# Pool product on two buffers with its low part one step later, and a fourth open unit in the attention output stage

## The reference

```python
# layer 0, four groups of 256 channels, windows 2, 4, 8, 16
u, gate = jnp.split(h @ w_in, 2, axis=-1)
pooled, new_hist = multiscale_pool(u, hist, hist_pos)
z = jnp.einsum('btgc,gcd->btgd', pooled, w_grp).reshape(B, T, POOL_WIDTH) * scale
y = (z * jax.nn.silu(gate)) @ w_out
# layer 1, 16 heads of 64, 4 key/value heads, window 128 in chunks of 64, with sinks
q, k, v, gate = jnp.split(h @ w_in, ...)
o = band_attend(q, k, v, qpos, kpos, sinks)
y = (o * jax.nn.silu(gate)) @ w_out
# both: x = x + gate_i(c) * y, with h = rms_norm(x) * (1 + scale_i(c)) + shift_i(c)
```

## Time and profile before

| | |
|---|---|
| median of three runs | 1714.47 us |
| the profiled execution's own time | 1710.07 us |
| its span, first to last instruction | 1708.1 us |
| mean granted TensorE clock | 0.964 |
| TensorE matmul busy | 1595.4 us, 9083 instructions |
| VectorE (DVE) busy | 866.5 us |
| ScalarE (ACT) busy | 747.4 us |
| GpSimd (POOL) busy | 420.2 us |

### The profile page before, as it was taken

The page is one execution under the profiler, slowest core; times in us unless marked ns, Lnnn a source line. Parts: engine busy times, 40 slices in busy tenths (PEclk is TensorE's granted clock), DMA queues, the critical chain, the costliest instruction groups (busy, mean ns, idle before and its releaser), DMA issues.

```text
span 1708.1 us, 27931 instructions
## 1 busy us (share of the span) xinstructions
PE 1595.4 (93%) x9083; PEld 1361.7 (80%) x9083; DVE 866.5 (51%) x2194; ACT 747.4 (44%) x1658; POOL 420.2 (25%) x403
## 2 busy tenths in 40 slices
PE   5899999999999999988888899999999999999998
PEld 3789987777777777788877788888788887888876
DVE  2555434433442444246666534677436765367751
ACT  3434332223222322246565543665545665456552
POOL 0333420011001100234434541233312333122331
PEclk8899999999999999999889889999999999999998
DMA  7777686556656655563434445433454334553323
GB/s 271 281 256 257 231 293 231 211 211 228 234 191 246 210 206 184 214 227 127 146 114 149 173 148 201 162 135 124 173 189 157 124 139 147 210 175 125 125 72 126
DMA packets 167605, 316.90 MB, mean 186 GB/s; under 512 B 21359, under 2 KB 88255, under 8 KB 167214
## 3 DMA queue, kind: packets, MB, share of 16 engines
q1 hardware_dynamic: 167470, 315.12, 52.7%
HBM read 240.96 MB, written 74.31 MB: 185 GB/s over the span
## 4 chain that ended last, share of the span: by engine, by line
PE 80%; DVE 6%; issue 4%; ACT 4%; DMA 1%; POOL 1%; SPq 0%; DVEq 0%; POOLq 0%; ACTq 0%
PE ps_u L832 65%; PE ps_o L1060 3%; PE ps_t L1033 3%; PE ps_s L1014 2%; PE ps_s L1015 2%; PE ps_s L863 1%; DMA work<-in_x_prompt_dram 1%; ACT work L1634 1%; DVE ps_u L1215 1%; ACT ps_u L1529 1%; PE ps_t L1073 1%; DVE ps_o L1393 1%; POOL work L1768 1%; DVE acc L1407 1%; PE ps_o L875 1%
## 5 line engine op out<-in xcount | busy, mean ns | idle before, releaser
L832 PE MATMUL ps_u<-h_all_hi,w_hi 128*128 128x512 f32 (+2 forms) x1440 | 525.2, 365 | 11.3 <-DVE acc L1224 6.3
L832 PE MATMUL ps_u<-h_all_lo,w_hi 128*128 128x512 f32 (+2 forms) x1440 | 515.6, 358 | 0.0
L832 PE MATMUL ps_u<-h_all_hi,w_lo 128*128 128x512 f32 (+2 forms) x1440 | 515.1, 358 | 0.0
L832 PEld LDWEIGHTS ps_u<-h_all_hi,w_hi 128*128 128x128 f32 x1440 | 279.8, 194 | 64.8 <-issue 17.8
L832 PEld LDWEIGHTS ps_u<-h_all_hi,w_lo 128*128 128x128 f32 x1440 | 278.9, 194 | 36.2
L832 PEld LDWEIGHTS ps_u<-h_all_lo,w_hi 128*128 128x128 f32 x1440 | 279.4, 194 | 34.4
L832 PE MATMUL ps_u<-y_hi,w_hi 128*128 128x512 f32 (+1 forms) x640 | 236.1, 369 | 12.8 <-POOL y_lo L1747 6.9
L832 PE MATMUL ps_u<-y_hi,w_lo 128*128 128x512 f32 (+1 forms) x640 | 230.3, 360 | 0.0
L832 PE MATMUL ps_u<-y_lo,w_hi 128*128 128x512 f32 (+1 forms) x640 | 230.1, 360 | 0.0
L1215 DVE TENSOR_TENSOR ps_u<-ps_u,rstd_b 128x512 f32<-128x512 f32 (+1 forms) x180 | 107.1, 595 | 208.1 <-PE ps_u L832 200.9
L1768 POOL TENSOR_TENSOR work<-work,recip 128x512 f32<-128x512 f32 (+2 forms) x136 | 132.9, 998 | 256.5 <-DVE recip L1380 256.5
(11 more groups left out here) (197 smaller groups left out, 2268.9 us busy)
## 6 DMA issues: line engine op xcount, KB each, us to landing
w_hi<-w_hi_kept SPq DMA_DIRECT2D x156, 512.0 KB, 3.6
w_lo<-w_lo_kept SPq DMA_DIRECT2D x156, 512.0 KB, 4.5
w_hi_kept<-w_hi SPq DMA_DIRECT2D x52, 512.0 KB, 2.7
w_lo_kept<-w_lo SPq DMA_DIRECT2D x52, 512.0 KB, 4.3
chunks<-in_ada_w_dram SPq DMA_DIRECT2D x32, 512.0 KB, 5.7
w_raw<-in_pool_w_in_dram SPq DMA_DIRECT2D x16, 512.0 KB, 5.6
w_raw<-in_attn_w_in_dram SPq DMA_DIRECT2D x16, 512.0 KB, 4.9
work<-in_x_prompt_dram SPq DMA_DIRECT2D x12, 512.0 KB, 6.0
```

The lines of the kernel that those rows point to most:

```text
L832: last = nc.tensor.matmul(out, w, x, start=(i == 0), stop=(i == n - 1))
```

## The change

The change has two parts.

*Pooling product.* The product for m = 1 is written to `sq`, that for m = 0 stays in `acc`. The subtraction that gives `y_lo` leaves step `E1` and becomes step `E2`, placed behind the `E1` of the following z unit. The wait of a z unit for the halves of the previous one is gone.

*Attention output stage.* Units get a bank by a rotation of their own, and the fourth unit opened in an attention output stage goes to the first bank of `ps_s`; in part 0 the fifth goes to the second. The plan opens four units (five in part 0) on slices 0 to 5 before the last item is through. Before it opens the fourth unit, TensorE waits until the scores have been read; the next stage's first use of `ps_s` waits for the readout of these units. A call that moved weight splits ahead (`split_to`) is kept for layer 0 alone there.

```diff
+            u = len(self.units)
+            if kind == "out" and more["layer"] and len(self.opened) in self.extra_banks(p):
+                bank = len(self.opened)
+            else:
+                bank = self.rotation
+                self.rotation = (self.rotation + 1) % 3
...
+    def extra_banks(self, p):
+
+        return (3,) if p else (3, 4)
...
                 for u in self.group(p, j, "z", n=2 * g + m, g=g, m=m):
                     self.project(u)
-                    s.extend(late)
+                    s.extend(late + lower)
+                    lower = [("E2", u - 1)] if late[0][0] == "E1" else []
                     late = [("E1", u)]
-            s.extend(late)
+            s.extend(late + lower + [("E2", late[0][1])])
...
+        top = 3 + len(self.extra_banks(p)) if layer else 3
...
-                for i in range(3):
+                for i in range(top):
                     self.project(order[i], done[i])
                     s.append(("E1", order[i]))
-                    self.split_to(j + AHEAD)
+                    if layer == 0:
+                        self.split_to(j + AHEAD)
...
-        plan = [(0, 0, 6), drain[0], (1, 0, 6), drain[1], (2, 0, 4), drain[2], (2, 4, 6)]
+        plan = [(0, 0, 6), drain[0], (1, 0, 6), drain[1], (2, 0, 6), drain[2], (3, 0, 6)]
         if p == 0:
-            plan.append(drain[3])
-        plan += [(0, 6, 7), drain[-1], (1, 6, 7), (2, 6, 7)]
+            plan += [drain[3], (4, 0, 6)]
+        plan += [(0, 6, 7), drain[-1], (1, 6, 7), (2, 6, 7), (3, 6, 7)]
...
+        def z_buf(u):
+
+            return sq if u["m"] else acc
...
-                    if u["u"] >= 3:
-                        v = units[u["u"] - 3]
+                    if u["bank"] >= 3:
+                        if k_from == 0 and u["bank"] == 3:
+                            claim("s", *[(x_new, x["nth_out"]) for x in units if x["s"] == u["s"] and x["bank"] >= 3])
+                    elif u["prev"] is not None:
+                        v = units[u["prev"]]
...
-                        if u["nth_z"] > 1:
-                            dve.wait_ge(yz_hi, u["nth_z"] - 1)
-                            dve.wait_ge(yz_lo, u["nth_z"] - 1)
-                        V.scalar_tensor_tensor(out=acc[:, c0:c0 + w], in0=bank[:, 0:w], scalar=half_ps[:, u["n"]:u["n"] + 1],
+                        V.scalar_tensor_tensor(out=z_buf(u)[:, c0:c0 + w], in0=bank[:, 0:w], scalar=half_ps[:, u["n"]:u["n"] + 1],
                                                in1=silu_g[:, i, c0:c0 + w], op0=ALU.mult, op1=ALU.mult).then_inc(y_ready, 1)
-                        dve.wait_ge(yz_hi, u["nth_z"])
-                        dve.wait_ge(y_ready, u["nth_z"])
-                        V.tensor_tensor(y_lo[:, u["n"], c0:c0 + w], acc[:, c0:c0 + w], y_hi[:, u["n"], c0:c0 + w].bitcast(F32),
-                                        ALU.subtract).then_inc(yz_lo, 1)
...
+                    if k == "z":
+
+                        dve.wait_ge(yz_hi, u["nth_z"])
+                        dve.wait_ge(y_ready, u["nth_z"])
+                        V.tensor_tensor(y_lo[:, u["n"], c0:c0 + w], z_buf(u)[:, c0:c0 + w], y_hi[:, u["n"], c0:c0 + w].bitcast(F32),
+                                        ALU.subtract).then_inc(yz_lo, 1)
```

More of the change, by code:

```diff
@@ L98, in __init__ @@
         self.stage = 0
+        self.rotation, self.last_in = 0, {}
         for p in range(PARTS):
@@ L141, in group @@
         for b, (c0, w) in enumerate(self.blocks(p)):
-            self.units.append(dict(u=len(self.units), s=self.stage, p=p, j=j, kind=kind, b=b, c0=c0, w=w, **more))
-            made.append(len(self.units) - 1)
+            u = len(self.units)
[4 more added lines that the diff above has]
+                self.rotation = (self.rotation + 1) % 3
+            if kind == "out" and more["layer"]:
+                self.opened.append(u)
+            self.units.append(dict(u=u, s=self.stage, p=p, j=j, kind=kind, b=b, c0=c0, w=w, bank=bank, prev=self.last_in.get(bank), **more))
+            self.last_in[bank] = u
+            made.append(u)
         self.last_unit[j] = made[-1]
@@ L221, in pool @@
                     s.append(("PL", p, g, 0))
-            late = []
+            late, lower = [], []
             for i in range(2):
@@ L275, in out_units @@
             us = self.group(p, j, "out", n=n, layer=layer)
-            fresh = us if len(order) >= 3 else us[3 - len(order):] if len(order) + len(us) > 3 else []
+            fresh = us if len(order) >= top else us[top - len(order):] if len(order) + len(us) > top else []
             before = len(order)
             order.extend(us)
-            if before < 3 <= len(order):
-                done = [0, 0, 0]
+            if before < top <= len(order):
+                done = [0] * top
                 for x in plan:
@@ L289, in out_units @@
                     if i == 0 and k0 == 0:
-                        self.split_to(j + (1 if p else 2))
-                for i in range(3):
+                        self.split_to(self.units[order[0]]["j"] + 3)
+                for i in range(top):
                     self.project(order[i], done[i])
                     s.append(("E1", order[i]))
-                    self.split_to(j + AHEAD)
+                    if layer == 0:
+                        self.split_to(j + AHEAD)
             for u in fresh:
@@ L546, in bank_of @@
         def bank_of(u):
-            return ps_u[u["u"] % 3][:, shifts(u):512]
+            return ps_u[u["bank"]][:, shifts(u):512] if u["bank"] < 3 else ps_s[:, u["bank"] - 3, :]
         def shifts(u):
@@ L936, in _ @@
                         pe.wait_ge(w_fetched[j % RING], 32 * fetches(j))
-                    bank = ps_u[u["u"] % 3]
+                    bank = ps_u[u["bank"]] if u["bank"] < 3 else ps_s[:, u["bank"] - 3, :]
                     slot = j % RING
@@ L1212, in _ @@
                         if p == 0 and u["b"] == 0:
-                            V.tensor_copy(wb[:, u["n"], :], ps_u[u["u"] % 3][:, 0:SHIFT])
+                            V.tensor_copy(wb[:, u["n"], :], ps_u[u["bank"]][:, 0:SHIFT])
                         dve.wait_ge(rb_ready, u["s"] + 1)
@@ L1556, in _ @@
                         act.wait_ge(y_ready, u["nth_z"])
-                        A(y_hi[:, u["n"], c0:c0 + w], acc[:, c0:c0 + w], ACT.Copy).then_inc(yz_hi, 1)
+                        A(y_hi[:, u["n"], c0:c0 + w], z_buf(u)[:, c0:c0 + w], ACT.Copy).then_inc(yz_hi, 1)
                     else:
```

3 lines of the change are left out of this document (2 added, 1 removed).

## The result

The changed kernel takes 1699.57 us at the median of four runs, beside 1714.25 for the kernel before (now also of four, hence not the 1714.47 above): a ratio of 0.9922, 95% interval 0.9902 to 0.9943. The forecast was 1705.0, within 1697 to 1712. A second comparison, further down, gave 0.9935 (0.9920 to 0.9950). The forecast's ratio, 0.9945, lies just outside the first interval and inside the second.

What follows compares the result with a forecast made beforehand. TensorE bounds the kernel, matmuls busy 93% of the span, so only its idle time and clock losses could shrink. Terms -8.2 - 4.3 - 3.1 + 6.1 = -9.5 us, from 1714.5 to 1705.0 us, range 1697 to 1712.

Steps and rivals of the forecast that it cites:

- Stage 0: Pooling z units: waits behind DVE's multiply go, three gaps of 2.09 us plus 1.9 of the fourth, together -8.2 us.
- Part 0: Attention's part 0: additional early matmuls fill the gaps, -4.3 us, and the clock holds, -3.1 us.
- Parts 1 to 3: Attention's later parts: +1.5 us each from less idle but a fetch stall, plus clock losses; together +6.1 us.
- the open point: Stage 0: second z multiply taken as free beside POOL's split, like L1215 at 0.44 us; if held, no gain.
- The fourth gap: Stage 0, before the output units: a 1.97 us wait, gain bounded by nothing and 2 us, taken as 1.9.
- the first rival: Stage 0: the DMA chain swallows the z gain, giving 2 to 3 of 8.2 us, about 1711; chance 0.2.
- The third 0.3: Part 0, third gap before the products with v: 18 more matmuls (2.25 us) leave 0.3 us of idle.
- The forecast counted 3.1: Part 0: the half-speed clock from 991.3 to 997.6 would hold instead, -3.1 us, bounds 0 and -3.9.
- 1.6 us before slice 7: Attention parts 1 to 3: TensorE idle of 1.6 us stays, from the end of slice 6 until slice 7 can start.
- 3.1 us of stall behind twelve matmuls: Attention parts 1 to 3, after slice 7: TensorE stands 3.1 us until the fifth weight tile lands.
- one fall of 1.7 us in each part: Attention parts 1 to 3: a clock loss of 1.7 us in every part, behind gaps of 1.6 and 3.1 us.
- what it counts as faster: Whole kernel faster than 1711.1 us: the forecast, the second rival and half of the first, given chance 0.82.

Runs made afterwards that it cites:

- A second comparison: The unaltered whole change measured again beside other kernels: 1705.30 us beside 1715.43 for the kernel before the change, ratio 0.9935.
- after: First profiled execution of the whole change against the kernel before it; median 1699.57 us beside 1714.25, ratio 0.9922.
- experiment 1: Only the z part of the change, on the kernel before with its three open units in attention: 1703.13 us beside 1713.06, ratio 0.9945.
- 2: Whole change, but additional open units in part 0 alone; parts 1 to 3 open three as before: 1695.56 us beside 1713.06, ratio 0.9894.
- Experiment 3: Whole change, but the fourth unit's 18 early matmuls in parts 1 to 3 are spread later: 1689.77 us beside 1713.06, ratio 0.9865.
- 5: The whole change run again, unaltered, against the kernel before: 1705.30 us beside 1715.43, ratio 0.9935.
- experiment 6: Whole change, but part 0 of attention opens four units instead of five: 1706.08 us beside 1715.43, ratio 0.9941.
- before: Profiled execution of the kernel without the change; median 1714.25 us in the first comparison.
- 4: Whole change with two buffers, but each y_lo right behind its multiply on VectorE as before: 1710.43 us beside 1713.06, ratio 0.9987.
- 7: Whole change with the old VectorE order, and the weight tile's split moved behind the group's last y_lo: 1709.41 us beside 1715.43, ratio 0.9966.
- Experiment 8: Kernel of Experiment 3 with each pool stage's third and fourth x tile loads earlier on SyncE's queue: 1684.70 us beside 1715.43, ratio 0.9824.
- 9: Kernel of Experiment 8, plus first loads of later output stages moved ahead of the first x_mid store: 1673.86 us beside 1713.16, ratio 0.9766.
- experiment 10: Kernel of 9, but products with the weights' upper half go first and the lower half is awaited behind them: 1668.20 us beside 1713.16, ratio 0.9731.

## Why the prediction came out

**The sum holds better than one execution shows.** Stage 0 with the new z order: 184.11, 181.69, 181.06, 179.68, 181.33 and 181.40 us (after, experiments 1 to 3, 5, 6), on average 181.5, against 188.57 before (and 188.50 with the old order in 4): -7.0 for a forecast of -8.2. Part 0 with five units: 297.58, 297.84, 297.75, 299.86 and 297.94 (after, 2 to 5), 298.2 on average against 305.20 and 304.60 (before, 1): -6.7 for -7.4. Parts 1 to 3 with the fourth unit as in the change: 666.45, 667.95, 672.19, 669.70 and 672.00 (after, 4 to 7), 669.7 against 665.37, 665.57 and 664.00 (before, 1, 2): +4.7 for +6.1. Together -9.0, and -9.5 was forecast. The median of the first comparison is 14.7 us lower, that of the second 10.1; the profiled executions differ by 11.7. The old order stands in few executions (two, two and three for the three stretches), and executions of one order differ by up to 4.4 us in stage 0 and 5.7 in parts 1 to 3, so the last microsecond of each difference means little.

**z: right, with one term too large.** Whether the multiply is held beside POOL's split had been the open point, and it hardly arose. In no execution, before or after, does a z multiply start beside a split: in the new order the second one is on its way 0.23 us before the split begins. It ends in its usual 0.49 us, and TensorE does not wait. That a multiply which starts behind the split's begin would also go through is still told only by L1215 in the earlier trace rows. The fourth gap was put at 1.9 of 0 to 2. It goes too, but the wait for x grows from 1.44 us to 2.4 to 4.2 (six executions, 2.9 on average), so 0.5 is left of it. This is the first rival's mechanism in small. It does not swallow the rest. Experiment 8 shows the cause, which I had named only in passing: the x load's late place on SyncE's queue.

**Part 0: right.** The idle went to 0.34, 0.58, nothing and 0.40 us for forecasts of 0.3, 0.8, 0.3 and 0.8, and the clock held. (The third 0.3 does not follow from the forecast's own terms: 2.25 us of matmuls cover a gap of 1.23 in full.) With 1.83 us of idle (experiment 6) its fall costs 1.7 us; with the gaps of up to 2.08 before it cost 5.1, and 3.4 in experiment 1, which has the old order there. The forecast counted 3.1.

**Parts 1 to 3: idle and stall right, the clock a mean of unlike cases.** 1.6 us before slice 7 was forecast and 1.63 measured; 3.1 us of stall behind twelve matmuls and 3.27, 2.85 and 2.89 measured (3.2 on average over the fifteen stalls of the five executions). I had counted one fall of 1.7 us in each part, 5.1 in all. After had one; the other four executions with the same order lost 5.1, 8.5, 6.8 and 8.5 us. The old order lost 3.4, 5.1 and 5.1. On average that is 6.1 against 4.5, and the difference is the 1.6 us of the forecast's sum (5.1 less 3.5). Of the fifteen stalls three left the clock up, six cost 1.7 us and six 3.4, and which did what does not follow their lengths: 3.44 us left it up, 2.92 cost 3.4. What decides it in a given execution stays open. The profiled execution of after is a lucky case. That such luck explains all that the first comparison gained beyond the forecast was not shown. The stretches hold falls of the clock in other places too, so the 1.4 us between +4.7 and +6.1 isn't resolved either. One slip in the forecast touches no time: the chances of what it counts as faster add to 0.80, not 0.82.

**The step not taken** was to ask how the early matmuls should be dealt out. The prediction had each piece: a chain that needs cover before slice 7, and a fetch that needs cover after it. Experiment 3 deals the same 18 matmuls out between the two and turns a cost of 4.7 us into a gain of 8.3 over the old order (656.7 against 665.0; experiments 8 and 9, with the same plan, have 655.5 and 656.7).

## What to carry to other kernels

Work moved ahead to fill one wait is taken from the cover of the next. Write down both waits with their lengths, and deal the work out between them; here 9 matmuls of cover behind unit 0 left a stall of 3.3 us, and 15 left 1.9. On a queue that takes its entries in order, look at what a load stands behind, above all at a store that waits for a result: the loads moved ahead in experiments 8 and 9 took the ratio from 0.9865 to 0.9766, some 17 us, more than the whole change. And where one fall of the clock costs 1.7 or 3.4 us and comes in one execution and not in the next, compare stretches over several executions before giving a difference a cause.

## What the runs showed of the hardware

- The same order of work, with stalls of 2.85 to 3.86 us, lost between 1.7 and 8.5 us to the clock over three output stages. A stall of 3.27 us left it at 1.00 once, and 2.85 us was followed by a fall in the same execution. In part 0 with five units no gap from the last products with v on was over 0.58 us, and in all nine executions the clock held from there to the end of the stage.
- DVE's y_lo, which starts 0.35 us behind the begin of POOL's split, takes 2.30 to 2.35 us and ends 0.3 us behind the split's end; without the split it takes 0.44. The Trainium skill ("SBUF — State Buffer", Who interferes with whom) states that a DVE instruction with two inputs in SBUF contends with a GpSimd instruction that reads SBUF, and the trace agrees. For the multiply, with one operand in PSUM, the trace agrees as far as it goes: it takes its usual 0.49 us where its last 0.26 us run beside the split.
- Two halves of 512 KB, issued 0.4 us apart at the head of a burst on one queue, let TensorE go on 3.7, 4.5 and 3.8 us after the first issue where only the first is waited for (experiment 10), and 4.9 to 5.9 us where both are (24 stalls of eight executions, after and experiments 3 to 9). In all 27 TensorE went on 0.09 us after the landing it needed.
